# A two-layer decoder step: the value products of every head split into rounded parts, the tensor engine's eight head turns written out, and one load moved

## The reference, cut to what matters

```
o = einsum('bgrqn,bngd->bqgrd', p, v)      # probabilities times values, f32
y = sum over branches of gates * o * silu(z)
```

## Time and profile before

| | |
|---|---|
| median of 3 runs | 2497.66 us (2497.07 to 2498.76) |
| the profiled execution | 2498.2 us |
| its span, first to last instruction | 2496.5 us |
| PE busy | 2437.5 us, 98% of the span |
| DVE, ACT, POOL busy | 901.1, 737.2, 372.3 us |
| the eight head turns | about 1233 to 2196 us from the span's start |

### The profile page before, as it was taken

The page is one execution under the profiler, slowest core; times in us unless marked ns, Lnnn a source line. Parts: engine busy times, 40 slices in busy tenths (PEclk is TensorE's granted clock), DMA queues, the critical chain, the costliest instruction groups (busy, mean ns, idle before and its releaser), DMA issues.

```text
span 2496.5 us, 49143 instructions
## 1 busy us (share of the span) xinstructions
PE 2437.5 (98%) x20790; PEld 2272.9 (91%) x20790; DVE 901.1 (36%) x1664; ACT 737.2 (30%) x1222; POOL 372.3 (15%) x505
## 2 busy tenths in 40 slices
PE   7999999999999999999999999999999999998997
PEld 6888888888899999999999999999898989977997
DVE  1236111221263353333533334333434333344433
ACT  1125111122232241111433333342433343432222
POOL 2002000790000000100411111111111111123000
PEclk9999999999999999999999999999999999999998
DMA  9985887676554345653532222323232323397222
GB/s 345 329 301 190 261 271 228 205 228 219 167 176 126 122 174 188 212 179 108 158 85 86 76 86 69 93 68 86 70 92 68 91 63 94 119 339 284 85 94 86
DMA packets 323401, 394.68 MB, mean 158 GB/s; under 512 B 20966, under 2 KB 287462, under 8 KB 320802
## 3 DMA queue, kind: packets, MB, share of 16 engines
q1 hardware_dynamic: 307554, 328.72, 41.5%
q0 software_dynamic: 15648, 62.97, 7.6%
HBM read 371.01 MB, written 42.69 MB: 166 GB/s over the span
## 4 chain that ended last, share of the span: by engine, by line
PE 93%; DVE 3%; ACT 2%; issue 1%; DMA 1%; POOL 0%; SPq 0%; ACTq 0%; DVEq 0%; POOLq 0%
PE acc L2033 71%; PE work L1948 4%; PE out_acc L2211 3%; PE work L1888 2%; PE work L2180 2%; PE work L2197 1%; PE work L2242 1%; PE acc L1888 1%; PE work L1936 1%; PE out_acc L2208 1%; PE acc L2255 1%; PE work L2174 1%; PE work L2119 1%; ACT probs L1176 0%; DMA w_c_early<-in_w_ck 0%
## 5 line engine op out<-in xcount | busy, mean ns | idle before, releaser
L2033 PE MATMUL acc<-h_hi,w_hi 128*128 128x260 f32 x4896 | 1009.6, 287 | 11.8 <-issue 8.9
L2033 PE MATMUL acc<-h_hi,w_lo 128*128 128x260 f32 x4896 | 986.5, 283 | 0.0
L2033 PE MATMUL acc<-h_lo,w_hi 128*128 128x260 f32 x4896 | 984.6, 283 | 0.0
L2033 PEld LDWEIGHTS acc<-h_hi,w_hi 128*128 128x128 f32 x4896 | 753.6, 189 | 51.7 <-issue 49.5
L1278 DVE TENSOR_TENSOR w_lo<-raw,w_hi 128x1024 fp32r<-128x1024 f32 (+1 forms) x316 | 403.9, 1279 | 1016.8 <-ACT w_hi L942 1013.4
L2033 PEld LDWEIGHTS acc<-h_hi,w_lo 128*128 128x128 f32 x4896 | 754.9, 189 | 0.0
L2033 PEld LDWEIGHTS acc<-h_lo,w_hi 128*128 128x128 f32 x4896 | 754.1, 188 | 0.0
L942 ACT ACTIVATE w_hi<-raw 128x1024 fp32r<-128x1024 f32 (+1 forms) x316 | 332.7, 1053 | 1117.3 <-PE acc L2033 1107.0
L892 POOL TENSOR_TENSOR probs<-probs,row_stats 128x128 f32<-128x128 f32 (+3 forms) x128 | 110.1, 889 | 451.5 <-DVE row_stats L1655 451.5
L1948 PE MATMUL work<-rows_T_early,w_c_early 128*128 128x124 f32 x960 | 114.5, 279 | 1.5 <-DMA w_c_early<-in_w_ck 1.5
L1948 PEld LDWEIGHTS work<-rows_T_early,w_c_early 128*128 128x128 f32 x960 | 112.1, 196 | 1.9 <-issue 1.9
(11 more groups left out here) (340 smaller groups left out, 1851.7 us busy)
## 6 DMA issues: line engine op xcount, KB each, us to landing
ada<-in_w_ada SPq DMA_DIRECT2D x192, 512.0 KB, 4.7
raw<-in_w_in_b SPq DMA_DIRECT2D x128, 512.0 KB, 3.8
raw<-in_w_in_a SPq DMA_DIRECT2D x64, 512.0 KB, 5.0
raw<-in_w_kv SPq DMA_DIRECT2D x48, 512.0 KB, 3.8
raw<-in_w_out_a SPq DMA_DIRECT2D x32, 512.0 KB, 3.6
raw<-in_w_out_b SPq DMA_DIRECT2D x32, 512.0 KB, 3.4
pages_early<-in_cache_k_cmp SPq DMA_DIRECT2D x32, 256.0 KB, 4.3
pages_early<-in_cache_v_cmp SPq DMA_DIRECT2D x32, 256.0 KB, 4.9
```

Of the source, the lines that this page charges most:

```text
L2033: last = mm_(out[half][0:n, 0:HT], part[slot][:, kk, cols_], src[:, k, half * HT:(half + 1) * HT], start=(first and part is HI and src is ...
```

## The change

1. The values of all branches become split parts. ACT writes `probs_T_hi` from all three banks (three copies in place of one), DVE writes `probs_T_lo` as bank minus hi (three subtractions and one copy of the last 128 columns, `probs_T_last`, in place of two copies; in the compressed branch one subtraction where DVE had nothing). PE makes three products for each of the blocks of 512, 384 and 256 columns; the block of 128 columns stays full float32.
2. Once a turn ACT (step 2) and DVE (step 3) split the values: `v_group_hi`, `v_group_lo`, `vc_group_hi`, `vc_group_lo`. For this ACT waits for the turn's loads (`hd_in`).
3. PE's `values` waits for `pt2_ready` alone beside `o_used`; the semaphores count 14 parts a turn. PE's `scores` for u > 2 waits bank by bank.
4. PE's eight turns are all written out. ACT's and DVE's stay as they were.
5. The samples' compressed values (`vc_sample`) are loaded by POOL in the sample stage and no longer at the first head turn, since their place in SBUF is now used by the heads.

```diff
             def turned(n, u):
                 act.wait_ge(b_done, n + 1)
                 wait(act, c_done, n)
                 if u < 2:
-                    nc.scalar.activation(PT[0:NCMP, 0:512], S[0][0:NCMP, :], ACT.Copy).then_inc(pt_ready, 1)
+                    nc.scalar.activation(PTH[0:NCMP, 0:512], S[0][0:NCMP, :], ACT.Copy).then_inc(pt_ready, 1)
                 else:
-                    nc.scalar.activation(PT[:, 0:512], S[0][:, :], ACT.Copy).then_inc(pt_ready, 1)
+                    for b, at, w in ((0, 0, 512), (1, 512, 384), (2, 896, 256)):
+                        last = nc.scalar.activation(PTH[:, at:at + w], S[b][:, 0:w], ACT.Copy)
+                        last.then_inc(pt_ready, 1)
...
+                    if s == 2:
+                        act.wait_ge(hd_in, 64 * (i + 1))
+                        wait(act, c_done, 6 * i)
+                        nc.scalar.activation(VCGH[:, :], VCG[:, :], ACT.Copy)
+                        nc.scalar.activation(VGH[:, :, :, :], VG[:, :, 0:NT - 1, :], ACT.Copy)
...
                 dve.wait_ge(b_done, n + 1)
-                dve.wait_ge(c_done, n)
-                V.tensor_copy(PT[:, 512:1024], S[1][:, :])
-                V.tensor_copy(PT[:, 1024:1280], S[2][:, 0:256]).then_inc(pt2_ready, 1)
+                wait(dve, c_done, n)
+                if u < 2:
+                    dve.wait_ge(pt_ready, parts(i, u) + 1)
+                    V.tensor_tensor(PTL[0:NCMP, 0:512], S[0][0:NCMP, :], PTH[0:NCMP, 0:512].bitcast(F32), ALU.subtract).then_inc(pt2_ready, 1)
+                    return
+                for b, at, w in ((0, 0, 512), (1, 512, 384), (2, 896, 256)):
+                    dve.wait_ge(pt_ready, parts(i, u) + b + 1)
+                    last = V.tensor_tensor(PTL[:, at:at + w], S[b][:, 0:w], PTH[:, at:at + w].bitcast(F32), ALU.subtract)
+                    if b == 1:
+                        last = V.tensor_copy(PT3[:, :], S[1][:, 384:512])
+                    last.then_inc(pt2_ready, 1)
...
+                    if s == 3:
+                        V.tensor_tensor(VCGL[:, :], VCG[:, :], VCGH[:, :].bitcast(F32), ALU.subtract)
+                        V.tensor_tensor(VGL[:, :, 0:NT - 1, :], VG[:, :, 0:NT - 1, :], VGH[:, :, :, :].bitcast(F32), ALU.subtract)
...
             def values(i, u):
                 n, br = 6 * i + u, u // 2
-                pe.wait_ge(pt_ready, n + 1)
-                if u >= 2:
-                    pe.wait_ge(pt2_ready, 4 * i + u - 1)
+                pe.wait_ge(pt2_ready, parts(i, u + 1))
                 wait(pe, o_used, n)
                 if br == 0:
-                    last = mm_(O[:, :], VCG[:, :], PT[0:NCMP, 0:512], start=True, stop=True)
+                    for v, p in ((VCGH, PTH), (VCGH, PTL), (VCGL, PTH)):
+                        last = mm_(O[:, :], v[:, :], p[0:NCMP, 0:512], start=(v is VCGH and p is PTH), stop=(v is VCGL))
                 else:
-                    for j, at in ((0, 0), (1, 512), (2, 1024), (3, 512 + 384)):
-                        last = mm_(O[:, P * j:512], VG[:, br - 1, j, :], PT[:, at:at + 512 - P * j], start=(j == 0), stop=(j == 3),
-                                   skip_group_check=True)
+                    for j, at in ((0, 0), (1, 512), (2, 896)):
+                        w = 512 - P * j
+                        for v, p in ((VGH, PTH), (VGH, PTL), (VGL, PTH)):
+                            mm_(O[:, P * j:512], v[:, br - 1, j, :], p[:, at:at + w], start=(j == 0 and v is VGH and p is PTH), stop=False, skip_group_check=True)
+                    last = mm_(O[:, P * 3:512], VG[:, br - 1, 3, :], PT3[:, :], start=False, stop=True, skip_group_check=True)
                 last.then_inc(c_done, 1)
...
-            looped(pe, o, 8, heads)
+            looped(pe, o, 8, heads, 8)
```

More of the change, by code:

```diff
@@ L399, in build, with parts @@
         assert c_norm_end + 2 * NKV * T * 4 <= keep_end
+        def parts(i, u):
+            return 14 * i + (u if u < 2 else 3 * u - 4)
         def bank(name):
@@ L2179, in scores @@
                     for t in (3, 2, 1, 0):
+                        if t and u > 2:
+                            pe.wait_ge(pt2_ready, parts(i, u) + 1 - t)
                         last = mm_(where[t], qs(t), kt_[:, :, 0:P * (t + 1)].rearrange("p o t -> p (o t)"), start=True, stop=True)
```

19 lines of the change are left out of this document (13 added, 6 removed).

## The result

| | before | after |
|---|---|---|
| median, five runs each | 2498.76 us (2497.07 to 2499.94) | 2484.92 us (2484.22 to 2487.58) |
| ratio, 95% interval | | 0.995 (0.994 to 0.9961) |
| the profiled execution, its span | 2498.2, 2496.5 us | 2484.45, 2482.8 us |

The kernel is 13.8 us faster (0.55%) by these two medians. The forecast was 2480.4 (17.3 faster); the result lies in its range and 4.5 us above its point.

The account below looks back on a forecast made before the run. TensorE's stream was taken as the bound. Savings of 11.9 + 2.9 + 6.2 = 21.0 us less losses of 3.5 + 0.2 = 3.7 gave 17.3 off 2498.2, 2480.9, or 2480.4 us as median; range 2471 to 2488 (forecast's own 2476 to 2486).

Parts of the forecast that it names:

- The value blocks: Units 2 to 5 of each head turn: nine split products shorten each block by 0.385 us, 11.9 us over 31 blocks.
- the upper bound (0.34): Value blocks: if a split product's surcharge grows with its width, the block takes 1.81 us and saves only 0.34.
- The compressed blocks: Units 0 and 1 of each head turn: three split products of 512 columns save 0.18 us each, 2.9 in all.
- the lower bound: Compressed blocks: 0.15 us saved each, if the surcharge of a split product grows with its width.
- the first rival: DVE isn't late at a turn's end and the row-count change cost vanishes with full precision: 2470.7 to 2477 us; chance 0.16.
- The branches: Ends of TensorE's looped turns: writing all turns out removes six gaps, saving 6.2 us.
- the rival: Turn ends: idle time is TensorE's code arriving, straight code has such gaps too, little returns: 2485.9 us; chance 0.10.
- The new wait at the end of a turn: Last value block waits for DVE's product of unit 4, 0.42 us late: 0.5 us a turn with fresh start, 3.5 lost.
- No wait at `scores`: After each unit's transposes: ACT's and DVE's copies free the S banks in time, first after 1.6 of 2.94 us.
- nothing new in the middle of a turn: Mid-turn, the softmax chain of DVE and ACT already ends late in looped turns and costs the same before and after.
- The load moved: Sample stage: POOL's load of vc_sample delays sets by 1.3 us, at most 3, but costs 0.2 us, bounds 0 and 1.5.

## Why the prediction was right, and where it was off

- **The value blocks: right, with two errors inside.** Between the kernel with only the turns written out and the kernel after, the heads fell from 933.42 to 923.32, 10.1 us; the forecast's terms for that are 11.9 + 0.4 (the block of the eighth turn) + 2.9 - 4.0 = 11.2. A block that starts afresh takes 1.80 for 2.15, saving 0.35 where I took 0.385; one that doesn't takes 1.72 for 2.07, the same 0.35. With the blocks and the wait as measured the sum is 32 x 0.35 + 16 x 0.16 - 4.0 = 9.8 of the 10.1 us. The extra cost of a split product isn't fixed, as I chose, but grows with its width: three of 512 columns take 0.70 us, a product of 260 takes 0.12, that is 0.00046 us a column for both. I had this as the upper bound (0.34). On the other side, the full-precision block of 128 columns takes 0.14 and not 0.215. By the rule of the Trainium skill (TensorE: Matmul & The Clock Gate, Back-to-back issue gap), which I had put beside it, a product of 512 columns would take 0.216; the trace has 0.233.
- **The compressed blocks: right, near the lower bound.** 0.16 us saved where I took 0.18, with 0.15 for a surcharge that grows with the width, which is what the trace has. The 0.2 us beyond the columns' own time stayed, so it doesn't belong to full precision; the first rival needed it to go.
- **The branches: right in size.** 6.5 us for 6.2 in the kernel with only this edit. What the rival said of the cause, that it is code arriving and not the branch as an instruction, has the branch records on its side: 3.3 to 5.2 us at these jumps, 0.21 to 0.24 in the short loop with the same branch line, and 16 KB of instructions that start to arrive 0.6 to 1.5 us into the record. No run tries it alone. But its conclusion, that straight code has such gaps too, is wrong for the heads: there are none in eight turns, although 16 KB of code arrive there every 16 us or so as well. The Trainium skill's 108 ns for a compare-and-branch (Advanced Engine Details and Errata, Control Flow Timing) are below all taken branches here, 0.21 us the shortest, and explain little of either.
- **The new wait at the end of a turn: right in size and cause.** 0.40 us late in the looped turns and 0.50 in the two others, for 0.42; with the afresh start 0.5 a turn, and the kernel that takes it away gains 4.0 us in eight turns.
- **No wait at `scores`, nothing new in the middle of a turn: right.** Neither appears among the waits.
- **The load moved: this term failed.** The step was "it delays the sets behind it by 1.3 us (0.5 MB at 400), at most 3 if 512-byte packets cost double", and then "I take 0.2 us, bounds 0 and 1.5". Measured by itself in the kernel before it costs 4.6 us. I had counted the bytes of the load and not what its small pieces do to the others: the rate falls to half for 11 us, sets land 6 to 8 us later, and the queue doesn't catch up before the last of them is used: that one still lands 4 us late, where the prediction had said no later than before. There is less slack than I read from the low slices of the earlier trace rows.
- **How much of the miss is the load.** Between the two profiled executions some 3.5 us are missing to the forecast: 0.8 in the heads, 3.5 in the sample stage, 0.9 in the first stretch, while the last stretch gave 1.8 us back that belong to the clock and not to the change. The other 1.0 of the 4.5 us lies between the profiled executions and the medians. In the sample stage the clock took no part (74.1 us busy for 74.3); TensorE stood idle 4.0 us longer. Of these 1.0 is the first wait. Leaving out seven eighths of the load takes away 1.5 us of idle time against the first profile of the kernel after and 0.7 against the second, and 1.1 to 1.4 us of the median. The rest, some 1.5 us, are "issue" gaps and waits for POOL: 6.2 us of them without the load, but 4.9 in the kernel before too and 5.8 in the one with only the turns written out, so this much may be scatter.
- **Why the load costs 4.6 us in the kernel before and 1.1 to 1.4 in the changed one** isn't settled. The medians' intervals are wide enough for a good part of it; the profile with the load moved has 2.2 of its 5.3 us from the lower clock; and where sets come early, waits for POOL and "issue" take up part of the time. Whether these gaps are code arriving was seen at single places and not tried, since no edit here changes when code arrives in that stage alone.
- **What no step had:** without the loop written out, the split values with their wait would have lost the gain. The branches' term was priced on the loop of before (6.5 us) and is worth 21.5 us in the changed kernel. The sum came out right because both edits were made; neither part's price could have been taken over to a kernel with one of them. The branch records show most of the reason: the new wait for DVE stands in front of the branch, so the branch starts 0.9 to 1.1 us later against the matmuls that used to cover it (5.9 us over six ends), the covering block is shorter (1.6), and four ends are followed by a halved clock (6.0). Why two of the branches last 4.7 and 5.2 us is open; the loop's body is longer than before by 28 matmuls a turn (six for each of four value blocks, two for each of two compressed ones), and no run shows whether that counts. That the forecast came out near is in this part luck: it had priced the wait and the loop's end as two separate terms.

## What to carry to other kernels

When an operand is split into more instructions on an engine, look first at what is queued behind the new instructions on that engine and raises a semaphore for another: here four instructions in place of two ahead of one product in each turn cost 4 us, and moving the product ahead gave them back. Price a load in a saturated stage by the size of its pieces as well as by its bytes, lay its source out in long rows, and look whether it takes anything from the stage at all by leaving it out. The price of a loop's end is not a constant of the loop: a wait in the last block before the jump also delays the jump, so that the work which hid it no longer does. Measure it again after each change of the body, and read the distance from last to first matmul there rather than the cause that the profile names. And before a stretch's length is called a gain or a loss, split it into idle and busy time and look at the granted clock over it.

## What the runs showed of the hardware that I had not expected

- The same 0.5 MB on the same queue lands in 17.7 us in pieces of 512 bytes and in 7.9 us in pieces of 4 KB, and halves the rate of all transfers (400 to 180 GB/s) for 11 us in the one case, and takes it to 254 for three in the other. From SP's queue at the same moment it delays the sets by as much, but with the DMA engines 20 to 40% busy for four us.
- The branch at the end of TensorE's long loop lasts 3.3 to 3.9 us in ten of twelve cases (4.7 and 5.2 in the others), where that of a short loop lasts 0.21 to 0.24. It cost 0.8 to 1.2 us a turn while the queue reached it 0.8 us ahead of the last block, and 2.0 to 4.0 where a wait held it back, while straight code of eight turns has no gap. Four of these six longer gaps were followed by a granted clock of 0.50 for 3.4 us.
- The same 1140 matmul records of the sample stage kept TensorE busy for 74.1 to 76.7 us, at a mean granted clock of 0.97 to 0.93.
- In a stage whose transfers are saturated TensorE can stop for up to 2.07 us in the middle of a run of matmuls on one buffer, with an instruction transfer of 16 KB under way.
